# A two-layer hybrid backbone: where VectorE normalises, how the state pass loads its rows, and which first rows are loaded a stage ahead

## What is computed

```python
def hybrid_layer(x, ctx, c, c_ctx, w_mod, b_mod, norm_g, w_in, w_out, ...):
    shift, scale, gate = jnp.split(jax.nn.silu(c) @ w_mod + b_mod, 3, axis=-1)
    h_lat = rmsnorm(x, norm_g) * (1.0 + scale[:, None]) + shift[:, None]
    s_lat = split_cols(h_lat @ w_in)
    branches = (mlstm_branch(...), diff_attn_branch(...), ssd_branch(...), hgrn2_branch(...))
    y_lat = jnp.concatenate([br[0] for br in branches], axis=-1) @ w_out
    x = x + gate[:, None] * y_lat

def finish(o, s):                      # HGRN2; the other branches end in like manner
    o = rmsnorm(o, norm_g.reshape(HG_HEADS, HG_DV))
    return o.reshape(*o.shape[:2], -1) * jax.nn.silu(s["hg_z"])
```

## Time and profile before

| | us |
|---|---|
| median of 3 runs (5918.35 to 5942.54) | 5933.59 |
| the profiled execution, its own time | 5931.59 |
| its span, first to last instruction | 5929.7 |
| PE busy | 5450.2 (92%) |
| DVE busy | 2914.2 (49%) |
| POOL busy | 2308.2 (39%) |
| ACT busy | 1675.7 (28%) |

### The profile page before, as it was taken

One profiled execution on the slowest core, in us unless ns is written; L12 is line 12 of the kernel. 1 busy time (PEld: TensorE's weight loads), 2 busy tenths in 40 slices (PEclk: granted clock), 3 DMA queues, 4 the chain that ended last, 5 costly groups with the idle time before them and its releaser, 6 DMA issues. The chain is left out here.

```text
span 5929.7 us, 74508 instructions
## 1 busy us (share of the span) xinstructions
PE 5450.2 (92%) x26120; PEld 2867.8 (48%) x26120; DVE 2914.2 (49%) x4926; ACT 1675.7 (28%) x4031; POOL 2308.2 (39%) x1695
## 2 busy tenths in 40 slices
PE   5999999967888799998999999999688879999989
PEld 2445454436777433332445544544467763333334
DVE  1444545434777655551113455455557766555212
ACT  1111111111444244444002212212123333444411
POOL 0112211113444279998001111111234435999910
PEclk7999999986999899999999999999779988999989
DMA  6232322247222100000623333332462220000032
GB/s 237 88 103 97 103 99 99 96 159 225 83 95 97 64 1 8 8 6 7 245 104 109 103 99 103 99 101 93 140 192 92 85 79 24 5 4 8 5 126 87
DMA packets 380770, 530.62 MB, mean 89 GB/s; under 512 B 109073, under 2 KB 266569, under 8 KB 374065
## 3 DMA queue, kind: packets, MB, share of 16 engines
q1 hardware_dynamic: 354690, 453.12, 23.1%
q10 hardware_dynamic: 19728, 40.41, 1.8%
q0 software_dynamic: 6048, 33.11, 1.5%
HBM read 372.13 MB, written 154.08 MB: 89 GB/s over the span
## 5 line engine op out<-in xcount | busy, mean ns | idle before, releaser
L607 PE MATMUL psum<-group_W,projection_hT 128*128 128x512 f32 (+4 forms) x5016 | 1954.9, 547 | 5.9 <-DVE projection_hT L729 5.7
L607 PEld LDWEIGHTS psum<-group_W,projection_hT 128*128 128x128 f32 x5016 | 951.2, 191 | 973.5 <-issue 932.0
L2266 POOL TENSOR_TENSOR attention_PS<-attention_PS 128x1024 f32<-128x1024 f32 x548 | 1265.8, 2351 | 83.6 <-ACT attention_PS L2399 75.9
L2312 DVE TENSOR_REDUCE attention_mxp<-psum 128x1 f32<-128x512 f32 (+1 forms) x1016 | 654.5, 686 | 543.4 <-PE psum L2448 543.4
L459 POOL TENSOR_TENSOR projection_cx<-projection_cx,projection_cw 128x768 f32<-128x768 f32 x102 | 186.8, 1831 | 1688.5 <-DMA projection_cw<-in_ss_conv_w 1688.5
L2399 ACT ACTIVATE attention_PS<-psum 128x512 f32<-128x512 f32 (+1 forms) x1168 | 630.6, 592 | 719.4 <-PE psum L2502 701.5
L2448 PE MATMUL psum<-attention_QK 32*128 32x512 f32 (+1 forms) x2592 | 772.6, 612 | 9.1 <-DVE attention_mxp L2301 6.1
L2496 PE MATMUL psum<-attention_QK 32*128 32x512 f32 x2336 | 665.6, 643 | 0.0
L2514 PE MATMUL psum<-attention_PS,attention_va 128*64 128x512 f32 x2336 | 628.9, 617 | 0.0
L680 ACT ACTIVATE projection_ut<-psum 128x256 f32<-128x256 f32 (+2 forms) x322 | 127.3, 406 | 1417.9 <-PE psum L607 1406.7
L2632 PE MATMUL psum<-output_W,output_yT 128*128 128x512 f32 x1088 | 478.5, 599 | 21.1 <-DMA output_W<-in_w_out 21.1
(11 more groups left out here) (361 smaller groups left out, 6151.5 us busy)
## 6 DMA issues: line engine op xcount, KB each, us to landing
u<-projection_ut SPq DMA_DIRECT2D x240, 256.0 KB, 2.0
projection_cx<-xbc SPq DMA_DIRECT2D x306, 128.0 KB, 2.2
projection_cw<-in_ss_conv_w SPq DMA_DIRECT2D x102, 384.0 KB, 4.4
mixing_hg<-u SPq DMA_DIRECT2D x34, 1024.0 KB, 5.1
group_W<-in_w_in SPq DMA_DIRECT2D x8, 2316.0 KB, 18.8
output_y<-y SPq DMA_DIRECT2D x34, 512.0 KB, 4.5
group_W<-in_w_in POOLq DMA_DIRECT2D x6, 2316.0 KB, 28.7
xbc<-projection_ut SPq DMA_DIRECT2D x34, 384.0 KB, 2.4
```

What stands on the lines that cost most here:

```text
L607: ins = nc.tensor.matmul(ps[n % RING][:, lo - c0:lo - c0 + w], hT[b][:, q], W[q][:, lo:lo + w], start=(q == 0), stop=(q == KT - 1))
L2266: G.tensor_tensor(SA[x % 2][:, rs, 0:w], one[:, rs, 0:w], PT[i % PTB][:, rs, 0:w], ALU.add) \
L2312: bk.release(V.tensor_reduce(mxp[x % 2][:, q:q + nn, 2 * pr + j, a], bk[job, j][:, 0:nn * (hi - lo)].rearrange("p (q n) -> p q n", q=nn), ...
```

## The change

In words, in the order of the stages. In `gates` the constant `pair` is loaded ahead of the bias and the six pieces. In `states` the forget gate and the input of HGRN2, which lie next to each other, come in one load (two strips in one load where a forward state is made), and keys and values of the mLSTM in one load `kv`; ACT copies the values into `va`, which has a column of ones between heads. At its end SP also loads the first `hg` rows of `mixing` and the first six tiles of `attention`, into two buffers that live as long as the group of these three stages; `gates` becomes a group of its own, so that its buffers are gone by then. In `mixing` `Y` has two buffers; DVE weights keys in round 2 and normalises at the end of round 4; POOL's `finish` comes in round 5, ACT's `store` in round 7. In `output` each piece of `w_out` has its own semaphore, TensorE multiplies both halves of the first tile piece by piece, and transposes the second tile after that.

```diff
 gates, SP
+                    sp.dma_start(pair[:], k.x["c_pair"]).then_inc(s["bias_in"], 16)
                     sp.dma_start(brow[:], ...)
                     for n in more:
                         sp.dma_start(wm[n][:], wl[:, :, n * 512:(n + 1) * 512]).then_inc(s[f"wm_in{n}"], 16)
-                    sp.dma_start(pair[:], k.x["c_pair"]).then_inc(s["bias_in"], 16)
 states
-    IN, RING, NLOAD = 4, 4, 7
+    IN, RING, NLOAD = 4, 4, 5
+    ALONG = CT + QG
...
+                        sp.wait_ge(s["spread"], n - IN + 1)
...
-                    for o, i in ((fi[b][:, 0:256], u[:, OFF["hg_f"] + d * 256:OFF["hg_f"] + d * 256 + 256]),
-                                 (fi[b][:, 256:512], u[:, OFF["hg_i"]:OFF["hg_i"] + 256]),
+                    f = OFF["hg_f"]
+                    rows = u[:, f + 256:f + 768] if d else u[:, f:f + 1024].rearrange("p (a n) -> p a n", a=2)[:, :, 0:256]
+                    for o, i in ((fi[b][:] if d else fi[b][:].rearrange("p (a n) -> p a n", a=2), rows),
+                                 (kv[b][:], u[:, 256:768]),
                                  (gt[b][:], k.gt[t]),
-                                 (key[b][:], u[:, 256:512]),
                                  (xb[b][:], k.xc[t, :, 0:512]),
-                                 (kk[b][:], ...),
-                                 (va[b][:, :, 0:64], u[:, 512:768].rearrange("p (h w) -> p h w", h=H))):
+                                 (kk[b][:], ...)):
                         sp.dma_start(o, i).then_inc(s[f"in{b}"], 16)
+                sp.dma_start(k.first_hg[:], k.u[CT if l == DEPTH - 1 else 0, :, OFF["ss_z"]:UW]).then_inc(k.first_in, 16)
+                sp.dma_start(k.ahead[:], k.u[0:ALONG, :, OFF["da_q"]:OFF["da_q"] + 512].rearrange("t p n -> p t n")) \
+                    .then_inc(k.ahead_in, 16)
...
                 for n in steps:
+                    loaded(act, n)
+                    if n >= IN:
+                        bk.wait(act, ("ml_hg", n - IN))
+                    nc.scalar.activation(va[n % IN][:, :, 0:64], h4(kv[n % IN][:, 256:512]), ACT.Copy).then_inc(s["spread"], 1)
                     bk.wait(act, ("sum", n))
...
                 def increments(n):
                     pe.wait_ge(s["weighted"], n + 1)
+                    pe.wait_ge(s["spread"], n + 1)
 mixing
-        Y = k.sb(c, "Y", [P, 3, 256])
+        Y = two("Y", [P, 3, 256])
 POOL
-                        if v == 4 and t:
-                            finish(t - 1)
                         if v == 5:
                             if t:
+                                finish(t - 1)
                                 gp.wait_ge(s["y_ready"], t)
 ACT
-                        if v == 5 and t:
+                        if v == 7 and t:
                             store(t - 1)
 DVE
-                        if v == 1:
+                        if v == 2:
                             bk.freed(dve, ("sum", t))
                             V.tensor_tensor(kh[:], hcol(t, "hg_k"), eh[:], ALU.mult).then_inc(s["kh_ready"], 1)
-                        if v == 2:
                             bk.wait(dve, ("S", t))
...
-                        if v == 3 and t:
-                            normalise(t - 1)
                         if v == 4:
...
                             bk.release(ins, ("CB", t))
+                            if t:
+                                normalise(t - 1)
                         if v == 5:
+                            if t >= 2:
+                                dve.wait_ge(s["y_ready"], t - 1)
...
-                            if t:
-                                dve.wait_ge(s["y_ready"], t)
 attention, PE
-                                pe.wait_ge(s[f"x_in{n}"], 16)
+                                pe.wait_ge(s[f"x_in{n}"] if n else k.ahead_in, 16 if n else 16 * (l + 1))
 output, PE
                 turn(0)
-                pe.wait_ge(s["w_in"], 16 * KT)
-                for n in range(N):
+                for a in range(2):
+                    bk.freed(pe, ("t", 0, a))
+                for q in range(KT):
+                    pe.wait_ge(s[f"w_in{q}"], 16)
+                    for a in range(2):
+                        ins = nc.tensor.matmul(bk["o", 0, a][:], yT[0][:, q], W[:, q, a * 512:(a + 1) * 512],
+                                               start=(q == 0), stop=(q == KT - 1))
+                        if q == KT - 1:
+                            bk.done(ins, ("o", 0, a))
+                turn(1)
+                for n in range(1, N):
```

More of the change, by code:

```diff
@@ L1217, in states @@
     TILES = [(0, t) for t in range(ahead)] + BACK
-    IN, RING, NLOAD = 4, 4, 7
+    IN, RING, NLOAD = 4, 4, 5
+    ALONG = CT + QG
     with ExitStack() as c:
-        key = [k.sb(c, f"key{b}", [P, 256]) for b in range(IN)]
+        kv = [k.sb(c, f"kv{b}", [P, 512]) for b in range(IN)]
         va = [k.sb(c, f"va{b}", [P, H, 65]) for b in range(IN)]
@@ L1447, in mixing @@
         og = three("og", [P, 2, 256])
-        hg = three("hg", [P, UW - OFF["ss_z"]])
+        hg = [k.first_hg] + [k.sb(c, f"hg{b}", [P, UW - OFF["ss_z"]]) for b in range(1, IN)]
         xc = three("xc", [P, XBC])
@@ L1565, in hg_loaded @@
             def hg_loaded(eng, t):
-                eng.wait_ge(s[f"hgin{t % IN}"], 16 * (t // IN + 1))
+                if t == 0:
+                    eng.wait_ge(k.first_in, 16 * (l + 1))
+                else:
+                    eng.wait_ge(s[f"hgin{t % IN}"], 16 * (t // IN + (t % IN > 0)))
             @block.gpsimd
@@ L2437, in keys @@
                         for a in range(4):
-                            ins = nc.tensor.transpose(k.bank[4 + t % 2][:, a * P:(a + 1) * P], xb[:, t, a * P:(a + 1) * P], k.ident[:])
+                            ins = nc.tensor.transpose(k.bank[4 + t % 2][:, a * P:(a + 1) * P], (xb if t >= CT + QG else k.ahead)[:, t, a * P:(a + 1) * P],
+                                                      k.ident[:])
                         ins.then_inc(s["key_mm"], 1)
@@ L2580, in output @@
         junk = k.sb(c, "junk", [P, D])
-        s = k.sems(c, "w_in gate_in y_in0 y_in1 y_in2 x_in0 x_in1 x_in2 scaled summed normed final stored0 stored1 act_step memsets")
+        s = k.sems(c, " ".join(f"w_in{q}" for q in range(KT)) + " gate_in y_in0 y_in1 y_in2 x_in0 x_in1 x_in2 scaled summed normed final stored0 stored1 act_step memsets")
         bk = Turns(k, c, uses)
@@ L2732, in build @@
         for l in range(DEPTH):
-            stages.append([(f"gates{l}", gates, (l,)), (f"states{l}", states, (l,)), (f"mixing{l}", mixing, (l,)),
+            stages.append([(f"gates{l}", gates, (l,))])
+            stages.append([(f"states{l}", states, (l,)), (f"mixing{l}", mixing, (l,)),
                            (f"attention{l}", attention, (l,))])
@@ L2741, in build @@
                 k.W = [k.sb(w, f"W{q}", [P, DIN]) for q in range(early)]
+                if group[-1][1] is attention:
+                    k.ahead = k.sb(w, "ahead", [P, CT + QG, 512])
+                    k.first_hg = k.sb(w, "first_hg", [P, UW - OFF["ss_z"]])
                 for name, f, args in group:
```

37 lines of the change are left out of this document (21 added, 16 removed).

## The result

The changed kernel takes 5967.74 us (median of 5 runs, 5964.04 to 5977.69), the kernel before 5930.9 us in the same comparison (5 runs). The ratio is 1.0068 with a 95% interval of [1.0052, 1.0085]: 0.7% slower, where 5861 us, 1.2% faster, was forecast. The profiled execution has a span of 5976.0 us.

The account below looks back on a forecast made before the run. TensorE, busy for 92% of the span, was taken as the bound, so only closing its gaps pays. Gains of 75.6 us less 4.8 lost took 5931.6 to 5860.8, say 5861; 5835 to 5890 held some 85%.

Parts of the forecast that it names:

- Mixing, its steady part: Mixing's 34 tiles: moved normalisation hidden, later `zg` meets DVE's division; +0.14 us a tile (-0.38 to +0.66), +4.8 in all.
- clock term for `output`: Rival: TensorE's clock stays low in output's first tile, +21 us, total 5882; 8%.
- one for `states`: Rival: denser work in states lifts the clock, steps go at the DMA's 3.3 us, 15 us less, 5846; 8%.
- The rival on the other side: Mixing: POOL's whole late block stands in DVE's division chain, 3.3 us a tile, +113 us, total 5969, slower; 4%.
- Of 3.2 us that leave DVE, 0.38 arrive: Mixing: without normalisation ahead, `Xq` starts 0.38 us sooner and shortens TensorE's wait for `num`: -0.38 us a tile.
- Gates: Gates: loading `pair` first ends TensorE's wait; work behind the biased products starts at 1276.75, gain 21.2 us once, bounds 18 and 22.
- States: States: five loads for seven, fewer packets, so steps fall from 4.34 to TensorE's 3.77 us; 8 us a layer, 16.
- The first rival: States: the DMA counts bytes, not packets, so only 2 of the 16 us remain, total 5875; 15%.
- low end of the sum: Five stage gains at their low ends, 18 + 12 + 4 + 14.2 + 12 = 60 us, giving 5876.
- Mixing's start: Mixing's start: `hg` loaded earlier, so weights come 3.4 us sooner in each layer, 6.8; bounds 2 and 3.6 a layer.
- Output: Output: products start piece by piece as `w_out` lands, second tile 8.0 us sooner, twice: 16; bounds 6 and 10.
- Attention: Attention's start: first six tiles already loaded, tiles 6 and 7 then limit; gain 7.8 us (7.1 to 8.5), twice: 15.6.

Follow-up runs that it names:

- filled gap: Changed kernel with TensorE making the six transposes of the next tile's HGRN2 queries and keys three times instead of once: 5906.42 us, 0.9958 of the kernel before.
- three delays: Kernel before with three useless DVE multiplications ahead of its drain of `ysum` in each tile of mixing: 6046.19 us, ratio 1.0184.
- all but the order: Changed kernel with mixing's old order and single `Y` restored, everything else as changed: 5876.2 us, 0.9907 of the kernel before.
- the 14 MB held back: POOL's next-projection load waits for output's third `y`; attention's lambda exponential also moved. Changed kernel with mixing's old order: 5872.97 us; with normalisation in round 3: 5877.01.
- early normalisation: Changed kernel with only DVE's normalisation put back in round 3 of mixing: 5882.24 us, 0.9912 of the kernel before.
- `zg` later: Changed kernel with POOL's three `zg` operations moved from round 5 to round 7, behind `ksT`: 5916.87 us, 0.9973 of the kernel before.
- one delay: Kernel before with one useless DVE multiplication ahead of its drain of `ysum` in each tile of mixing: 5955.1 us, ratio 1.0032.
- order alone: Kernel before with only the changed order of mixing, including two `Y` buffers, all loads as before: 6025.81 us, ratio 1.0149.

## Why the prediction was wrong

The step that failed is "Mixing, its steady part": +0.14 us a tile, +4.8 in all. The measured loss is 85.6 us in the two stages, or some 92 beside the 6.4 won at their starts.

- Its mechanism of the collision was right, and its upper end came near: +0.66 "if `den` meets two of the three `zg` operations and the division's product one", and 0.63 was measured at full clock. That the two agree so well is in part luck. The terms given (twice the 0.37 by which `den` grows, and 0.2, less 0.38) add up to 0.56. The rows show a loss of 1.22, and the product met an `Xk` and not a `zg`. What is lost in the chain also didn't "count in full": 0.30 and 0.28 of it came off TensorE's waits for `num` and `Aw`. I took the middle of -0.38 and +0.66 because single rows showed both kinds of meeting. The order of the operations settles which it is: POOL runs `yo` and `zg` back to back behind the normalisation, so the time of the whole block follows from one end. I put the block 1 us later, and it came 1.2 us later against DVE's chain, but I didn't work out what it meets there, nor that the normalisation would take 1.48 us beside the two `Xk`, for which `yo` waits 0.90.
- What was missing altogether is the clock, 2.8 us a tile and most of the loss. I carried a clock term for `output` and one for `states`, but put the clock at nothing in the mixing, as it stood at 1.00 there. Yet TensorE's wait of 1.39 us is in each tile, and the price of a longer one is not its length. With the filled gap this was shown by taking the wait away, and with the three delays by making it. The rival on the other side had the size (3.3 us a tile) but from a wrong mechanism, all of POOL's block in DVE's chain; it had 4%.
- "Of 3.2 us that leave DVE, 0.38 arrive": right. The wait for `num` fell by 0.3 us a tile.
- Gates: the work behind the products starts at 1277.18 for 1297.92, 20.7 us sooner (20.2 counted from the stage's start), for 21.2 forecast. The stage in this profile is only 12.4 us shorter, since much of its work ran at the lower clock: the last 32 products with `pair` took 6.99 us, and 3.73 in the run of all but the order. Seven of the nine profiles with the new loads have 63.2 to 65.1 us, 19 to 21 below the 83.9 of before, and two have 71.0 and 71.5; the old gates took 86.7 to 87.2 in three other profiles. The range of 18 to 22 holds for the seven against the 83.9.
- States: 16 forecast, 4.0 measured. The packets were taken for what counts, from two rates, 277 and 388 GB/s, of loads that differ in other ways too. The rule of the Trainium skill ("DMA: Bandwidth & Descriptors", section "Why small descriptors are slow (HBM only)") gave, by an estimate from its figure, some 4.5% off a step's DMA work. The trace is nearer to it than to my 24%: the step is 3.4% shorter in this profile (16 steps from the first sums: 68.9 us to 66.5), and 2.0 and 0.5% in two others with the same loads. The first rival, with 2 us, was nearer than the forecast; its 2 us were also the lower bound that I gave for this term, and the low end of the sum has 12 in their place.
- Mixing's start: 3.4 forecast for each layer, 3.6 and 2.8 measured. Output: 8.0 forecast for each, 8.9 and 9.2 measured at the second tile's start, of which the first layer gave back 5.7 by the end of its stage; with the 14 MB held back, the stage was 5.2 us shorter.
- Attention: 7.8 forecast for each layer, 4.4 and 3.8 measured at the first score product. I had let ACT's evictions slow the transposes, but overlooked that ACT stands first for lambda, whose wait was hidden before behind that for the keys. A stall that is removed shows what stood behind it.

Without the mixing's order the forecast of the rest was 75.6 us and 54 were measured, 12 of the difference in the states and some 7 in attention.

## What to carry to other kernels

A wait of a half idle engine, however large in the list, is worth what arrives at the bound engine: here 79 us of DVE's waits were worth 10 (the wait for `num`), and the order that was to use them cost 95. Before lengthening any wait of TensorE, look at the clock behind its longest regular gap: here 1.2 us more of waiting cost 3.4 in a tile, and useless products in the gap were cheaper than the gap. And when the end of one operation moves, follow everything queued behind it on the other engine to the next place where the two meet.

## What the runs showed of the hardware

- TensorE's granted clock fell from 1.00 to 0.50 at single short waits, in work in which TensorE is otherwise busy. The table counts, in windows of 1 us, the falls that begin under the wait for `ysum` or within 2 us behind it (the last tile of each layer is left out, and its first stands by itself):

| kernel | wait, us | falls at it |
|---|---|---|
| filled gap | 1.1 to 1.3 | 0 of 30 |
| before | 1.1 to 1.4 | 0 of 30 |
| early normalisation | 1.5 | 0 of 30 |
| first tiles of six kernels | 1.57 | 5 of 12 |
| `zg` later | 1.6 to 1.7 | 7 of 30 |
| one delay | 1.8 to 1.9 | 0 of 20 |
| one delay, two of them first tiles | 2.0 to 2.1 | 4 of 4 |
| changed | 2.5 to 2.6 | 26 of 30 |
| order alone | 2.5 to 2.6 | 29 of 30 |
| three delays, two of them first tiles | 2.9 to 3.4 | 28 of 32 |

- The length of the wait does not settle it: equal waits came with and without a fall in one run, and the falls in the middle of the tile (eleven with one delay, ten with three, one in the kernel before) follow waits of under 1 us. What decides among them stays open.
- Where a two-input operation of DVE met one of POOL, even eight columns paid: `den` took 0.58 and 0.64 us beside `zg` instead of 0.17.
- In the states 45% fewer packets at the same bytes shortened the first layer's step by 3.4% in one profile and by 2.0 and 0.5% in two others.
